# Seven stage borders of a transformer kernel: the first block by token halves, the second half turned in between

## The reference

```
h = layer_norm(x, ln_in_g, ln_in_b)
for layer in range(2):
    rq, rk, rv, rg, hq, hf, hi, hg, sq, sk, sv, ga, gb, gc = split(h @ w_in[layer])
    merged = sigmoid(ga)*retention(rq, rk, rv, rg) + sigmoid(gb)*hgrn(hq, hf, hi, hg) + sigmoid(gc)*window_attention(sq, sk, sv)
    h = layer_norm(a*h + merged @ w_o[layer])             # a = 4 ** 0.25
    ff = swiglu(h)  if layer == 0 else  top-2 mixture of 8 experts(h)
    h = layer_norm(a*h + ff)
```

## Time and profile before

| | us |
|---|---|
| median of three runs | 3395.19 |
| the profiled execution | 3397.42 |
| its span in the profile | 3395.6 |
| TensorE matmuls busy | 3198.0 |
| VectorE busy | 2254.2 |
| ScalarE busy | 1867.5 |
| TensorE idle before the turns of h: for L736 / for L691 | 32.6 / 9.3 |

### The profile page before, as it was taken

The page is one execution under the profiler, slowest core; times in us unless marked ns, Lnnn a source line. Parts: engine busy times, 40 slices in busy tenths (PEclk is TensorE's granted clock), DMA queues, the critical chain, the costliest instruction groups (busy, mean ns, idle before and its releaser), DMA issues.

```text
span 3395.6 us, 41644 instructions
## 1 busy us (share of the span) xinstructions
PE 3198.0 (94%) x15948; PEld 2667.5 (79%) x15948; DVE 2254.2 (66%) x2659; ACT 1867.5 (55%) x2444; POOL 14.4 (0%) x26
## 2 busy tenths in 40 slices
PE   6999889999999979999899899996999999999997
PEld 5888468787987867888688787875888788788885
DVE  4549855555445564656555647565898898898886
ACT  4442254544445434646444446463777677677774
POOL 0000000000000000000000000000000000000000
PEclk9999999999999989999899999997999999999998
DMA  8444265554526444533454344334999899999993
GB/s 272 166 146 149 75 198 168 188 196 154 151 79 226 143 147 156 191 124 149 161 186 173 138 158 157 133 126 158 347 358 359 328 358 357 336 358 357 346 360 137
DMA packets 381149, 719.10 MB, mean 212 GB/s; under 512 B 14009, under 2 KB 153727, under 8 KB 380831
## 3 DMA queue, kind: packets, MB, share of 16 engines
q1 hardware_dynamic: 376368, 707.71, 58.6%
q0 software_dynamic: 2368, 8.52, 0.7%
q10 hardware_dynamic: 2223, 0.31, 0.1%
HBM read 715.44 MB, written 1.05 MB: 211 GB/s over the span
## 4 chain that ended last, share of the span: by engine, by line
PE 87%; DVE 7%; ACT 4%; issue 1%; DMA 0%; ACTq 0%; DVEq 0%; POOL 0%; SPq 0%
PE duo L981 13%; PE duo L983 13%; PE duo L982 13%; PE acc L981 8%; PE acc L983 8%; PE acc L982 8%; PE aux L981 2%; PE aux L983 2%; PE aux L982 2%; PE duo L542 1%; PE duo L387 1%; PE duo L544 1%; PE duo L543 1%; PE aux L542 1%; PE aux L544 1%
## 5 line engine op out<-in xcount | busy, mean ns | idle before, releaser
L1540 DVE TENSOR_TENSOR weights_split<-w,weights_split 128x1024 fp32r<-128x1024 f32 x672 | 791.6, 1221 | 120.6 <-ACT weights_split L1519 110.3
L1519 ACT ACTIVATE weights_split<-w 128x1024 fp32r<-128x1024 f32 x672 | 677.4, 1057 | 253.6 <-PE duo L983 177.5
L981 PE MATMUL duo<-weights_split,u_high 128*128 128x512 f32 x1776 | 705.3, 397 | 8.8 <-DVE weights_split L1540 5.7
L983 PE MATMUL duo<-weights_split,u_low 128*128 128x512 f32 x1776 | 694.8, 391 | 0.0
L982 PE MATMUL duo<-weights_split,u_high 128*128 128x512 f32 x1776 | 694.3, 391 | 0.0
L416 DVE TENSOR_TENSOR w_low<-w,w_high 128x1024 fp32r<-128x1024 f32 x304 | 368.4, 1223 | 348.2 <-ACT w_high L407 347.5
L1098 DVE TENSOR_TENSOR weights_split<-w,weights_split 128x1024 fp32r<-128x1024 f32 x320 | 377.6, 1221 | 283.4 <-ACT weights_split L1086 283.2
L407 ACT ACTIVATE w_high<-w 128x1024 fp32r<-128x1024 f32 x304 | 317.9, 1056 | 364.3 <-PE acc L983 99.0
L1086 ACT ACTIVATE weights_split<-w 128x1024 fp32r<-128x1024 f32 x320 | 322.3, 1058 | 256.2 <-PE duo L983 155.3
L981 PEld LDWEIGHTS duo<-weights_split,u_high 128*128 128x128 f32 x1776 | 335.9, 189 | 83.1 <-issue 8.8
L982 PEld LDWEIGHTS duo<-weights_split,u_high 128*128 128x128 f32 x1776 | 335.8, 189 | 71.1 <-issue 2.9
(11 more groups left out here) (401 smaller groups left out, 5022.9 us busy)
## 6 DMA issues: line engine op xcount, KB each, us to landing
w<-in_ffn_w_dram SPq DMA_DIRECT2D x132, 1024.0 KB, 7.6
w<-in_moe_w_gate_dram SPq DMA_DIRECT2D x112, 1024.0 KB, 7.1
w<-in_moe_w_up_dram SPq DMA_DIRECT2D x112, 1024.0 KB, 6.9
w<-in_moe_w_down_dram SPq DMA_DIRECT2D x112, 1024.0 KB, 8.1
w<-in_w_in_dram SPq DMA_DIRECT2D x92, 1024.0 KB, 7.1
w<-in_hyb_w_in_dram SPq DMA_DIRECT2D x18, 1024.0 KB, 7.2
w<-in_ffn_w_gate_dram SPq DMA_DIRECT2D x11, 1024.0 KB, 7.5
w<-in_ffn_w_up_dram SPq DMA_DIRECT2D x11, 1024.0 KB, 9.9
```

Of the source, the lines that this page charges most:

```text
L981: pe.matmul(bank_out, x_hi, w_hi, start=first, stop=False, skip_group_check=True)
L983: return pe.matmul(bank_out, x_lo, w_hi, start=False, stop=last, skip_group_check=True)
L1519: act.activation(units[:, place, 0, cut], src[:, cut], ACT.Copy).then_inc(sem("moe_high"), 1)
L1540: m = dve.tensor_tensor(units[:, place, 1, cut], src[:, cut], units[:, place, 0, cut], ALU.subtract)
```

## The change

1. `pe_turn_h`, `act_turned_split` and `dve_turned_split` take a part of the four groups, (0, 1) for token half 0 and (2, 3) for half 1.
2. Dense stages: the first block's `up` is `up_first`. It turns half 0, runs its 24 matmuls (x = 0, then x = 1), turns half 1 and runs its 24. `unit_used0` comes with the third twelve instead of the second. ScalarE and VectorE split unit 1 between the two halves of u.
3. Retentions: the first block is rv's first one, token-major, by halves (`pe_first_block_tm`): three pieces of half 0, the turn of half 1, the fourth piece, then the four pieces of half 1, which free them. rq, rk, rv 1 and rg follow. The weight loads and the feeds are reordered to match.
4. The layer norms before ff0 and before the retentions call the split of half 0 (in ff0 with unit 1) between half 1's statistics and its L733.
5. The rms norm behind ffn11 and the layer norm ln_in are joined, half by half. The gain row of ln_in goes to a free part of u (`first_gain`) and its bias to `rows[:, 1, :]`, both issued at the start of ffn11.

The core of the diff:

```
+        def act_postnorm_root(key, t):
+            act.wait_ge(sem("sumsq"), at("sumsq", (key, 2 * t + 1)))
+            act.wait_ge(sem("first_sum"), at("first_sum", (key, t)))
+            act_root((key, t), rot[:, 2 + t:3 + t], ssq[:, 5 + 2 * t:6 + 2 * t], ssq[:, 2 + t:3 + t])
...
             for t in range(NT):
+                if key == "ln_in":
+                    dve_postnorm("ffn11", 0.5, "ln_in", (t,))
                 statistics(t)
+                if t and between is not None:
+                    between()
                 V(dve.scalar_tensor_tensor(out=h[:, t, :], in0=h[:, t, :], scalar=mv[:, 2 * t:2 * t + 1],
-                                           in1=rows[:, 0, :], op0=ALU.subtract, op1=ALU.mult))
+                                           in1=first_gain if key == "ln_in" else rows[:, 0, :], op0=ALU.subtract, op1=ALU.mult))
...
+        def act_layernorm(key, between=None):
+            if key != "ln_in":
+                act_root_table()
             for t in range(NT):
+                if key == "ln_in":
+                    act_postnorm_root("ffn11", t)
+                    if t == 0:
+                        act_postnorm_sums("ffn11", 1)
                 act.wait_ge(sem("variance"), at("variance", (key, t)))
                 act_root((key, t), rot[:, t:t + 1], mv[:, 2 * t + 1:2 * t + 2], eps5)
+                if t == 0 and between is not None:
+                    between()
...
         def pe_dense(key, fm_key, total, body):
+            pe_turn_h(fm_key, (0, 1))
...
+            def up_first():
+                for t in range(NT):
+                    if t:
+                        pe_turn_h(fm_key, (2, 3))
+                    claim(4 + t)
+                    cut = slice(t * P, (t + 1) * P)
+                    for x in range(2):
+                        pe.wait_ge(sem("fm_split"), at("fm_split", (fm_key, 2 * t + x)))
+                        pe.wait_ge(sem(f"unit_split{x}"), split0[x] + 1)
+                        whi, wlo = (units[:, x, y, :].rearrange("p (t n) -> p t n", n=COLS) for y in range(2))
+                        for k in range(4):
+                            m = products(bank(4 + t), uh[:, 4 * x + k, cut], ul[:, 4 * x + k, cut],
+                                         whi[:, k, :], wlo[:, k, :], first=(x == 0 and k == 0),
+                                         last=(x == 1 and k == 3))
+                        if x == 1:
+                            m.then_inc(bank_full(4 + t), 1)
+                        elif t == 1:
+                            m.then_inc(sem("unit_used0"), 1)
...
         def act_dense_prenorm(key, row):
             if key == "ffn00":
                 act_first_unit(key)
-            act_turned_split((key, "pre"), lambda c: pcol("norm_g", row * 8 + c))
+            act_turned_split((key, "pre"), lambda c: pcol("norm_g", row * 8 + c), (0, 1))
             act_unit(key, 1, 0, 0, 4)
+            act_turned_split((key, "pre"), lambda c: pcol("norm_g", row * 8 + c), (2, 3))
...
+        def pe_first_block_tm(key, h_key):
+            banks = next_pair(key)
+            halves = []
+            for t in range(NT):
+                if t == 0:
+                    pe_turn_h(h_key, (0, 1))
+                claim(banks[t])
+                cut = slice(t * P, (t + 1) * P)
+                for p in range(4):
+                    if t == 0:
+                        halves.append(pe_piece())
+                    high, low = halves[p]
+                    pe.wait_ge(sem("fm_split"), at("fm_split", (h_key, 2 * t + p // 2)))
+                    for k in (2 * p, 2 * p + 1):
+                        cols_of = slice((k % 2) * COLS, (k % 2 + 1) * COLS)
+                        m = products(bank(banks[t]), uh[:, k, cut], ul[:, k, cut], high[:, cols_of], low[:, cols_of],
+                                     first=(k == 0), last=(k == KC - 1))
+                    if t == 0 and p == 3:
+                        m.then_inc(bank_full(banks[0]), fill(banks[0], key))
+                    if t == 0 and p == 2:
+                        pe_turn_h(h_key, (2, 3))
+                    if t:
+                        piece_done(m)
+            filled_by_piece(banks[1], key)
...
         def pe_retention(l):
             first_pair()
-            pe_block_fm((l, "rq"), fm_key=("h", l), halves=True)
+            pe_first_block_tm((l, "rv", 0), ("h", l))
+            pe_block_fm((l, "rq"))
...
+                if key == "ffn11":
+                    pool_rows("ln_in", prev, a["ln_in_g_2"], a["ln_in_b_2"], first_gain)
                 pool_rows(key, prev, a["norm_g"][layer, g + 1])
...
-                wcols(0, 512, 1024, 1536, 2048, 2560, 8704, 9216)
+                wcols(1024, 0, 512, 1536, 2048, 2560, 8704, 9216)
```

More of the change, by code:

```diff
@@ L658, in dve_prenorm, with act_postnorm_sums @@
                     .then_inc(sem("normed"), mark("normed", (key, t)))
+        def act_postnorm_sums(key, t):
+            for half in range(2):
+                i = 2 * t + half
+                full_wait(act, 3 if key == "mixA" else i, key)
+                m = act.activation(junk[:, t, half * 512:(half + 1) * 512], acc[:, i, :], ACT.Square,
+                                   scale=D ** -0.5, accum_out=ssq[:, 4 + i:5 + i])
+                m.then_inc(sem("sumsq"), mark("sumsq", (key, i)))
+        def act_postnorm_root(key, t):
+            act.wait_ge(sem("sumsq"), at("sumsq", (key, 2 * t + 1)))
+            act.wait_ge(sem("first_sum"), at("first_sum", (key, t)))
+            act_root((key, t), rot[:, 2 + t:3 + t], ssq[:, 5 + 2 * t:6 + 2 * t], ssq[:, 2 + t:3 + t])
         def act_postnorm(key):
@@ L663, in act_postnorm, with dve_postnorm @@
             for t in range(NT):
[L664 to L676, removed]
+                act_postnorm_sums(key, t)
+                if key != "ffn11":
+                    act_postnorm_root(key, t)
+                elif t == 0:
+                    return
+        def dve_postnorm(key, factor, next_key, part=range(NT)):
+            if 0 in part:
+                dve.wait_ge(sem("rows_landed"), at("rows_landed", key))
+            for t in part:
                 for half in range(2):
@@ L689, in dve_postnorm, with dve_layernorm @@
                 dve.wait_ge(sem("acc_scaled"), scaled)
-                part = h_part(next_key, t) if next_key != "ln_in" or t else ("ln_in", "first")
+                h_key = h_part(next_key, t) if next_key != "ln_in" or t else ("ln_in", "first")
                 dve.scalar_tensor_tensor(out=h[:, t, :], in0=hn[:, t, :], scalar=rsd[:, 4 + t:5 + t], in1=h[:, t, :],
-                                         op0=ALU.mult, op1=ALU.add).then_inc(sem("h_ready"), mark("h_ready", part))
-        def dve_layernorm(key, with_acc, next_key):
+                                         op0=ALU.mult, op1=ALU.add).then_inc(sem("h_ready"), mark("h_ready", h_key))
+                if next_key == "ln_in":
+                    dve.wait_ge(sem("h_ready"), latest("h_ready"))
+        def dve_layernorm(key, with_acc, next_key, between=None):
             if with_acc == "experts":
@@ L1002, in up @@
                     for t in range(NT):
[L1003 to L1007, removed]
+                        if x == 0:
                             pe.wait_ge(sem("hidden_ready"), hid0 + 2 * j + t + 1 + 2 * body * i)
@@ L1210, in turned_at, with pe_turn_h @@
             return (6, 7, 0, 1)[i]
-        def pe_turn_h(key):
-            for i in range(4):
+        def pe_turn_h(key, part=range(4)):
+            for i in part:
                 t, b = i // 2, turned_at(i)
@@ L1221, in pe_turn_h, with act_turned_split @@
                 m.then_inc(bank_full(b), fill(b, (key, i)))
-        def act_turned_split(key, gain):
-            for i in range(4):
+        def act_turned_split(key, gain, part=range(4)):
+            for i in part:
                 t, b = i // 2, turned_at(i)
@@ L1232, in act_turned_split, with dve_turned_split @@
                 m.then_inc(sem("fm_high"), mark("fm_high", (key, i)))
-        def dve_turned_split(key, gain):
-            for i in range(4):
+        def dve_turned_split(key, gain, part=range(4)):
+            for i in part:
                 t, b = i // 2, turned_at(i)
```

67 lines of the change are left out of this document (36 added, 31 removed).

## The result

The changed kernel takes 3411.70 us, the median of four runs (3409.53 to 3416.38), against 3393.47 for the kernel before on the same chip (four runs). The ratio is 1.0057, with a 95% interval of 1.0045 to 1.0069: 18.2 us slower. The profiled execution took 3411.54 us for a span of 3409.6, 14.0 more than the span of before. The two differences are not the same number because the profiled execution of before, 3397.42, lies 4.0 above its median.

The account below looks back on a forecast made before the run. TensorE, busy 3198.0 of 3395.6 us, bounds the kernel. 17.5 + 1.1 - 8.4 - 3.3 = 6.9, plus 4.4 of clock, 11.3 slower: 3408.7 profiled, less 2.2 for the median, 3406.5 (3397 to 3414).

Parts of the forecast that it names:

- Dense stages, 17.5: Four rms dense stages: open chain after half 1's turn and later hidden turn lose 5.0, 3.8, 4.9 and 3.8, 17.5 us together.
- The two extra terms: Added losses: 0.6 at ffn10 for the second weight unit, wanted earlier; 0.8 at ffn00 for one more ScalarE table load.
- ff0, 1.1: At ff0: open chain 2.65, silu 1.1 and low clock 0.7, less a start 3.3 earlier: 1.1 us lost.
- h0, 8.4: At retention h0: no wait for layer-norm rows, first matmul 9.5 earlier, some given back: 8.4 us won.
- h1, 3.3: At retention h1: only what lies behind half 1's statistics moves; 4.8 earlier, some given back: 3.3 us won.
- The sum without the clock, 6.9: Whole kernel: dense stages and ff0 lost, less h0 and h1 won, 6.9 us slower at an unchanged clock.
- The clock, 4.4: Ten new TensorE idles in dense stages and ff0; three followed by a clock drop costing 1.45 each: 4.4 us.
- Rival 1: The clock stays at 2.4 GHz in all ten new idles: 3402.1 us; chance 0.22.
- Rival 2: Dense stages: ScalarE and VectorE overlap the second half's chain, 4.0 lost instead of 17.5; faster, 3386 us; chance 0.06.
- Rival 3: Retentions: weight pieces held over both halves make TensorE wait at the next block, 1 to 2 each; 3409.5 us; chance 0.12.

Follow-up runs that it names:

- Kernel 1: The changed kernel with all five dense stages back in the old order; retentions, joined norms and early rows stay changed: 3380.3 us.
- Kernel 4: The changed kernel with 8 added unused matmuls behind the second turn and 8 ahead of the hidden turn in all five dense stages: 3398.6 us.
- kernel 3: The changed kernel with the second turn put behind the first 12 of half 0's 24 matmuls in the four rms dense stages: 3395.7 us.
- kernel 2: The kernel before with the new order by token halves in the four rms dense stages alone: 3419.8 us.

## Why the prediction was right, and where its sizes were off

The forecast was slower, 3406.5 (3397 to 3414); measured 3411.7. Its steps in the order of the text:

- **Dense stages, 17.5.** From the first turn to the hidden turn ffn00, ffn01, ffn10 and ffn11 take 5.26, 4.08, 7.04 and 6.91 more than before. Each matmul that starts at the slow distance costs 0.20 of that; there are 5, 2, 16 and 15 more of them. What is left is 4.3, 3.7, 3.8 and 3.9, in all 15.7 against 5.0, 3.8, 4.9 and 3.8. The idle of 2.0 came as worked out, to a tenth. The hidden turn was to wait 2.3 (5.3 less 2.72 and the tail of 0.29); it waits 1.84 at ffn10 and 2.12 to 2.24 at the other three. The two extra terms, 0.6 for the second unit at ffn10 and 0.8 for the table load at ffn00, did not show: no wait stands ahead of half 0's second twelve at ffn10, and the hidden turn at ffn00 waits 2.21. In both places a low stretch (from 668.4 and from 40.4) had slowed the matmuls just ahead, so the terms can be hidden in it; what they are at the full clock is open.
- **ff0, 1.1.** 1.74 more, of which 8 slow matmuls make 1.6. The idles are 1.40 and 2.02, as the chain without gains and silu say.
- **h0, 8.4.** The first turn is 9.2 earlier, measured from ffn11's hidden turn; 7.24 lie between it and the first matmul (7.3 forecast). No wait for rows is left on VectorE: the statistics of half 0 (1237.92) start 0.04 behind the rms step, where the earlier trace rows has 6.65. The order on ScalarE cost what was said of it. The high parts of half 0 start 1.15 behind the turn and half 1's root follows them:

```profile
1243.63 1.64 ACT L1277 ACTIVATE u_high<-aux 128x128 fp32r<-128x128 f32 x8 [3.72 <-PE aux L1265]
1245.13 0.32 ACT L623 ACTIVATE small<-small 128x1 f32<-128x1 f32 x1
```
```profile
1245.48 0.16 DVE L628 RECIPROCAL small<-small 128x1 f32<-128x1 f32 x1 [1.79 <-ACT small L623]
1245.68 1.28 DVE L703 SCALAR_TENSOR_TENSOR h<-arena,small,h 128x1024 f32<-128x1024 f32 x1
...
1248.69 1.68 DVE L1288 SCALAR_TENSOR_TENSOR u_low<-aux,u_high 128x128 fp32r<-128x128 f32 x8
```

  The gain up to the end of the third block is 7.5.
- **h1, 3.3.** 3.2 from the first turn of h1 to the turn that follows its layer. Kernel 1 has 10.9 in the rest for both retentions.
- **The sum without the clock, 6.9.** 5.4 in the rest. Part of that nearness is luck: the loss at the dense stages was put 1.8 too high and the win at h0 0.9 too high, and the two misses work against each other.
- **The clock, 4.4.** 8.6: the step of the forecast that was mis-sized. It counted ten new idles, three of them with a drop of 1.45. Five had one: low stretches begin within 1.5 of 39.73, 49.30, 677.15, 1052.98 and 1712.25, and none does at the idles of 480.95, 488.91, 686.29, 1062.40 and 1704.54. Two places more lie at the wait of half 0 for its low parts, 2.71 at ffn10 and 2.65 at ffn11. Before, the turn of half 1 had stood in it, and the forecast did not count it as an idle. At ffn10 the low stretch is new (from 668.4); at ffn11 before has one of 3.4 already (from 1024.7), and now it is 6.8 long (from 1040.5). A drop is 1.7 by my count, the longer stretch 1.1 more, in all 11.3; other places of the kernel had 2.7 less than before. Kernel 4 fills the ten idles, and with the five drops 8.5 of clock go; its other 9 are not tied to them.
- **Rival 1** (the clock stays, 3402.1) is out by the same rows, and with it the rule of the Trainium skill, "TensorE: Matmul & The Clock Gate", section "Why this matters for your kernels", as a bound: idles of 1.95 to 2.71, below the length that it asks to avoid, had a new drop behind them in six places. **Rival 2** (the chain hidden) is out by the idles of 2.0; kernel 3 shows what it would take, other matmuls in its place. **Rival 3** (held pieces) is out: kernel 1 came in 0.7 below its range, and in the first block and the next TensorE waits 0.05 at most for a piece.

From 11.3 forecast to 14.0 in the profile is -1.5 in the rest and +4.2 in the clock. The medians say 18.2, 4.0 of the difference being the profiled execution of before. Which way the drops fall differs from run to run: kernel 2 alone spreads over 12.

What stays open is why, at idles of the same length, the clock falls behind one and not behind the other. Kernel 3 has the same wait at ffn10, 2.70, and all 48 matmuls behind it at the full clock. Such places, and the two stretches of the experts that swapped, suggest that it changes with when the program gets there; no run tests that by itself.

## What to carry to other kernels

Work by halves pays where the second half's wait has something else to stand in it. At the retentions TensorE had been waiting for the norm anyway; at the four rms dense stages half 1 had kept it waiting 1.62 at most, and the split opened a chain of 3.1 between two runs of matmuls. If it must be split, put the second turn into the first half's matmuls rather than behind them: in kernel 3 that took back 16.0, and the time was then the old order's again. And count as a new idle also the one in which some other instruction used to stand.

## What the runs showed of the hardware

- More than half of the time that a change costs can lie in TensorE's clock: 8.6 of the 14.0 between the two profiles, by a count that is safe to a few us. Idles of 1.95 to 2.71 had drops behind them, and others of the same length (2.00 and 2.24 at ffn01, 2.70 at ffn10 in kernel 3) had none.
- Removing a low stretch paid only where TensorE worked in it. Filling idle time that is itself at the low clock raised the mean granted clock (0.56 to 0.74) and left h0's first 48 matmuls at 14.9. Filling short idles amid steady matmuls won 13.1 by the medians, although the waits stayed and TensorE did 80 matmuls more; about half of the clock part that went lay at the filled places.
